# Query and key chunks of the input projection: one 512-column product for both halves of x, partial sums added on VectorE, bias preparation in other units

## What is computed

```python
xn = rms_norm(h, ln1_w)
proj = xn @ w_in          # 9 chunks of 512 columns: q, k, v of 3 attention groups; then GLA q, k, v, gate; merge gates
o_a = dilated_mixer(a_qkv)
o_b = gla_mixer(gq, gk, gv, gog, glr, w_gk2, b_gk2, gla_norm_w)
mixed = gate_a * (o_a @ w_proj_a) + gate_b * (o_b @ w_proj_b)
h = h + mixed @ w_out
h = h + moe_ffn(rms_norm(h, ln2_w), ...)      # top 4 of 32 experts, each 1024 -> 2048 -> 1024
```

## Time and profile before

| | us |
|---|---|
| three runs, median (lowest to highest) | 1250.7 (1250.55 to 1251.64) |
| span of the profiled execution, first to last instruction | 1248.5 |
| TensorE busy | 1169.1 (94%) |
| VectorE busy | 445.6 (36%) |
| ScalarE busy | 250.3 (20%) |
| GpSimd busy | 15.9 (1%) |

### The profile page before, as it was taken

How to read it: one execution, slowest core, us unless ns; L and a number is a source line. 1 busy time by engine, 2 the same in 40 slices (tenths; PEclk the granted TensorE clock), 3 DMA queues, 4 the chain that set the end, 5 groups by cost and what they waited for, 6 DMA issues and landing times.

```text
span 1248.5 us, 17019 instructions
## 1 busy us (share of the span) xinstructions
PE 1169.1 (94%) x7215; PEld 604.2 (48%) x7216; DVE 445.6 (36%) x766; ACT 250.3 (20%) x353; POOL 15.9 (1%) x30
## 2 busy tenths in 40 slices
PE   9999999999999999899899989898989989899997
PEld 9998988888633343333333333333333333333332
DVE  5754546666532233222222222222322222222232
ACT  4544445544401010001000000000000001000012
POOL 2200000000000000000000000000000000000000
PEclk9999999999999999999999999999999999999999
DMA  9645333377999999999999999999999999999996
GB/s 296 219 169 186 135 135 135 135 277 282 371 417 425 431 431 427 430 430 429 431 433 427 431 430 429 430 430 434 433 428 431 433 427 431 435 427 432 421 428 278
DMA packets 50031, 456.98 MB, mean 366 GB/s; under 512 B 5988, under 2 KB 6136, under 8 KB 31400
## 3 DMA queue, kind: packets, MB, share of 16 engines
q1 hardware_dynamic: 49544, 455.09, 87.7%
q10 hardware_dynamic: 448, 1.32, 0.3%
HBM read 455.35 MB, written 1.05 MB: 366 GB/s over the span
## 4 chain that ended last, share of the span: by engine, by line
PE 59%; DMA 35%; DVE 2%; SPq 2%; ACT 1%; issue 1%; DVEq 0%
PE ps L1384 57%; DMA ring<-in_w_up_dram 22%; DMA arena<-in_w_up_dram 12%; PE ps L1891 1%; DMA ring<-in_w_in_dram 1%; ACT w_split L588 0%; SPq L397 0%; DVE w_split L892 0%; SPq L399 0%; PE ps L1777 0%; PE ps L1573 0%; SPq L414 0%; DVE arena L1062 0%; SPq L391 0%; PE ps L1680 0%
## 5 line engine op out<-in xcount | busy, mean ns | idle before, releaser
L1384 PE MATMUL ps<-ring,arena 128*64 128x512 f32 x2304 | 523.2, 608 | 50.9 <-DMA ring<-in_w_up_dram 50.9
L1384 PEld LDWEIGHTS ps<-ring,arena 128*64 128x64 f32 x2304 | 163.9, 140 | 378.8 <-issue 300.3
L1384 PE MATMUL ps<-arena 128*64 128x512 f32 (+3 forms) x920 | 202.7, 563 | 17.0 <-DMA arena<-in_w_up_dram 16.1
L1296 DVE TENSOR_SCALAR arena<-ps 128x512 f32<-128x512 f32 x32 | 22.1, 692 | 487.3 <-PE ps L1384 487.3
L892 DVE TENSOR_TENSOR w_split<-ring,w_split 128x2048 fp32r<-128x2048 f32 x48 | 109.8, 2291 | 108.4 <-ACT w_split L588 108.1
L1384 PEld LDWEIGHTS ps<-arena 128*64 128x64 f32 (+1 forms) x920 | 78.2, 149 | 128.4 <-issue 100.2
L796 ACT ACTIVATE arena<-arena 128x512 f32<-128x512 f32 x32 | 20.2, 631 | 552.6 <-DVE arena L1296 552.6
L1384 PE MATMUL ps<-w_split,x_split 128*128 128x512 f32 x528 | 123.5, 392 | 0.7 <-ACT arena L624 0.5
L1384 PEld LDWEIGHTS ps<-w_split,x_split 128*128 128x128 f32 x528 | 98.4, 188 | 21.8 <-issue 1.2
L588 ACT ACTIVATE w_split<-ring 128x2048 fp32r<-128x2048 f32 x47 | 89.6, 1911 | 70.7 <-PE ps L1384 62.5
L1384 PE MATMUL ps<-x_split,w_split 128*128 128x256 f32 x768 | 94.7, 284 | 0.1
(11 more groups left out here) (251 smaller groups left out, 624.8 us busy)
## 6 DMA issues: line engine op xcount, KB each, us to landing
ring<-in_w_up_dram SPq DMA_DIRECT2D x40, 4096.0 KB, 31.1
ring<-in_w_down_dram SPq DMA_DIRECT2D x46, 2048.0 KB, 30.2
arena<-in_w_up_dram SPq DMA_DIRECT2D x14, 4096.0 KB, 31.1
ring<-in_w_in_dram SPq DMA_DIRECT2D x17, 2048.0 KB, 7.8
arena<-in_w_down_dram SPq DMA_DIRECT2D x14, 2048.0 KB, 30.0
ring<-in_w_up_dram SPq DMA_DIRECT2D x12, 2048.0 KB, 23.1
arena<-in_w_up_dram SPq DMA_DIRECT2D x4, 2048.0 KB, 23.5
ring<-in_w_up_dram SPq DMA_DIRECT2D x8, 1024.0 KB, 8.7
```

The costliest lines, as they stand in the source:

```text
L1296: dve.tensor_scalar(glu_c, ps[bank][:, :], LIMIT, None, ALU.min).then_inc(glu_ok, 1)
L1384: return pe.matmul(dst, lhsT, rhs, start=start, stop=stop, skip_group_check=True)
```

## The change

1. The two halves of x lie side by side for each k tile: `x_both` is [P, KT, 2, SEQ]; `x_split` is the same memory with the axes swapped back.
2. In the seven chunks 1, 3, 4, 6, 7, 9, 10 (`by_weights`, 14 units) the high weights multiply both halves of x in one matmul of 512 columns, into a whole bank: columns 0 to 255 hold high x high, 256 to 511 high x low. Low weights x high x is a second matmul of 256 columns into the first half of the bank. A unit of chunks 3 to 10 so fills two banks, ps[0] and ps[1], one for each of its two groups of 128 columns (m), and the next unit uses the same two (`bank_free`). Chunk 1 uses ps[2] to ps[5].
3. VectorE adds the two halves of a bank and writes the result (`halves_added`, TENSOR_REDUCE, 256 sums of two), 28 of them; ScalarE's 14 copies of these chunks go. `halves_added(u)` stands ahead of w_low(u+3).
4. The bias preparation stands in other units: pieces of u = 6 and 7 in 10, of 8 in 11, of 9 in 16, and the small split of 10 in 12. Those of u = 4 and 5 stay.
5. The semaphore `warmed`, on which nothing waits, goes.

```diff
+        x_both = nc.alloc_sbuf_tensor_at("x_split", [P, KT, 2, SEQ], F32R, offset=slot_at[DENSE_RING])
+        x_split = x_both[:, :, :, :].rearrange("p k i t -> p i k t")
...
+        def by_weights(u):
+            return u // 2 == 1 or (u // 2 < QKV_CHUNKS + 2 and u // 2 not in BY_ROWS)
...
+        def dve_outs(u):
+            return sum(2 for v in range(u) if by_weights(v))
...
                 if u == 5:
                     then(dve.tensor_tensor(bias_f, bias_f, bias_p[0:E, :], ALU.subtract))
-                if u == 6:
+                if u == 10:
                     then(dve.tensor_copy(tmp_b, bias_f))
-                if u == 7:
                     dve.tensor_copy(bias_p[E:2 * E, :], tmp_b)
-                if u == 8:
+                if u == 11:
                     then(dve.tensor_tensor(bias_f, bias_f, tmp_b, ALU.subtract))
-                if u == 9:
+                if u == 16:
                     dve.tensor_copy(bias_p[2 * E:3 * E, :], bias_f).then_inc(pick_ok, 1)
-                if u == 10:
+                if u == 12:
                     dve.wait_ge(glr_in, 32)
...
+            def halves_added(u):
...
+                for m in range(2):
+                    if m == 0:
+                        dve.wait_ge(tile_done, halves_done(u))
+                    else:
+                        dve.wait_ge(proj_done, u + 1)
...
+                    dve.tensor_reduce(dst, ps[m].rearrange("p (i t) -> p t i", i=2), AX_X, ALU.add).then_inc(added, 1)
...
+            def bank_free(u, b):
+                if by_weights(u - 1) and u != 4:
+                    pe.wait_ge(added, dve_outs(u) - 1 + b)
+                else:
+                    pe.wait_ge(proj_out, act_outs(u) - 1 + b)
...
-                if u >= 2:
-                    pe.wait_ge(proj_out, u - 1)
                 for m in range(2):
-                    dst = ps[u % 2][:, m * SEQ:m * SEQ + SEQ]
+                    bank_free(u, m)
                     for k in range(KT):
-                        ins = product(dst, [split_w(u, i)[:, k, m * P:m * P + P] for i in range(2)],
-                                      [x_split[:, i, k, :] for i in range(2)], k == 0, k == KT - 1)
-                ins.then_inc(proj_done, 1)
+                        w = [split_w(u, i)[:, k, m * P:m * P + P] for i in range(2)]
+                        mm(ps[m], w[0], x_both[:, k, :, :].rearrange("p i t -> p (i t)"), k == 0, False)
+                        ins = mm(ps[m][:, 0:SEQ], w[1], x_split[:, 0, k, :], False, k == KT - 1)
+                    ins.then_inc((tile_done, proj_done)[m], 1)
```

More of the change, by code:

```diff
@@ L263, in layer @@
         res_ok = [sem(f"res_ok{t}") for t in range(TT)]
-        wo_half, part_ok, sel0_ok, xin_half_ps, xin_half_ok, warmed = (
-            sem(n) for n in ("wo_half", "part_ok", "sel0_ok", "xin_half_ps", "xin_half_ok", "warmed"))
+        wo_half, part_ok, sel0_ok, xin_half_ps, xin_half_ok = (
+            sem(n) for n in ("wo_half", "part_ok", "sel0_ok", "xin_half_ps", "xin_half_ok"))
         lg_ps, lg_shift, lg_exp, taken_ok, count_ps, turns_ok = (
@@ L316, in split_w, with act_outs, tiles_before, halves_done @@
             return w_split[:, u % SPLITS, part, :].rearrange("p (k n) -> p k n", k=tiles)
+        def by_weights(u):
+            return u // 2 == 1 or (u // 2 < QKV_CHUNKS + 2 and u // 2 not in BY_ROWS)
+        def act_outs(u):
+            return sum(1 for v in range(u) if not by_weights(v))
+        def dve_outs(u):
+            return sum(2 for v in range(u) if by_weights(v))
+        def tiles_before(u):
+            return sum(1 for c in BY_ROWS if c < u // 2) + sum(1 for v in range(4, u) if by_weights(v))
+        def halves_done(u):
+            return tiles_before(u) + 1
         def tiles_done(c):
-            return BY_ROWS.index(c) + 1
+            return tiles_before(2 * c) + 1
         O_BANK = ((5, 2), (6, 7))
@@ L625, in projection_out @@
                     return
-                if c < DENSE_RING:
+                if c == 0:
                     if s == 0:
@@ L636, in projection_out @@
                     return
[L637 to L648, removed]
             def mix_high(j):
@@ L1084, in gate_products @@
                        .then_inc(gl_ops, 1)
+            def halves_added(u):
+                c, s = u // 2, u % 2
+                if c == 1:
+                    if s:
+                        for m in range(4):
+                            if m < 2:
+                                dve.wait_ge(tile_done, tiles_done(c))
+                            else:
+                                dve.wait_ge(proj_done, u + 1)
+                            dve.tensor_reduce(qkT[:, 1, 0, m, :], ps[2 + m].rearrange("p (i t) -> p t i", i=2),
+                                              AX_X, ALU.add).then_inc(added, 1)
+                    return
+                for m in range(2):
+                    if m == 0:
+                        dve.wait_ge(tile_done, halves_done(u))
+                    else:
+                        dve.wait_ge(proj_done, u + 1)
+                    if c < QKV_CHUNKS:
+                        dst = qkT[:, c % 3, c // 3, 2 * s + m, :]
+                    else:
+                        if u == 2 * C_GQ and m == 0:
+                            dve.wait_ge(pick_ok, 1)
+                        dst = (gqT if c == C_GQ else gkT)[:, s * 512 + m * SEQ:s * 512 + m * SEQ + SEQ]
+                    dve.tensor_reduce(dst, ps[m].rearrange("p (i t) -> p t i", i=2), AX_X, ALU.add).then_inc(added, 1)
             for u in range(UNITS):
+                if by_weights(u):
+                    halves_added(u)
                 if U_PB <= u < U_WO and (u - U_PB) % 2:
@@ L1470, in projection @@
                     for m in range(4):
-                        if first and m % 2 == 0:
-                            pe.wait_ge(proj_out, m // 2 + 1)
                         for k in range(4):
                             kk = 4 * (u % 2) + k
-                            ins = product(ps[m // 2][:, m % 2 * SEQ:m % 2 * SEQ + SEQ],
-                                          [split_w(u, i)[:, k, m * P:m * P + P] for i in range(2)],
-                                          [x_split[:, i, kk, :] for i in range(2)], kk == 0 and m % 2 == 0, kk == KT - 1)
+                            w = [split_w(u, i)[:, k, m * P:m * P + P] for i in range(2)]
+                            mm(ps[2 + m], w[0], x_both[:, kk, :, :].rearrange("p i t -> p (i t)"), kk == 0, False)
+                            ins = mm(ps[2 + m][:, 0:SEQ], w[1], x_split[:, 0, kk, :], False, kk == KT - 1)
                         if m == 1 and not first:
@@ L1484, in projection @@
                     for t in range(TT):
-                        if first and u + t >= 2:
-                            pe.wait_ge(proj_out, u + t - 1)
+                        if first:
+                            bank_free(u, t)
                         for k in range(4):
@@ L1556, in at_scores @@
                 if h == 0:
-                    pe.wait_ge(proj_out, 2 * QKV_CHUNKS)
+                    pe.wait_ge(proj_out, act_outs(2 * QKV_CHUNKS))
+                    pe.wait_ge(added, dve_outs(2 * QKV_CHUNKS))
                 for g in range(NG):
```

21 lines of the change are left out of this document (11 added, 10 removed).

## The result

| | kernel before | changed kernel |
|---|---|---|
| median of five runs each, us | 1250.55 (1250.23 to 1251.64) | 1260.61 (1259.12 to 1261.22) |
| ratio, 95% interval | | 1.0073 (1.0062 to 1.0084) |
| span of the profiled execution, us | 1248.5 | 1259.5 |

The change costs 10.1 us; 7.7 were forecast. In a later session (experiment 11) it was 1262.93 against 1250.81, ratio 1.0093 (1.0073 to 1.0112), so 12.1 us.

What follows compares the result with a forecast made beforehand. TensorE was taken to bound the projection, transfers the experts, with dense-part losses carried to the end. Gain -2.2, waits +6.9 and slow clock +3.0 gave +7.7 us on 1250.7: 1258.4 us, range 1254.0 to 1262.0.

Steps and rivals of the forecast that it cites:

- Cost 3: Units 6 and 12: sums stand behind 3.34 us bias subtractions on VectorE, so TensorE idles 3.5 and 3.4 us, 6.9 together.
- Cost 2: VectorE's sums take 0.69 us each and fit in plain query units with 0.3 us left over.
- the rival of double sums: VectorE's sums cost 1.38 us each, lengthening both waits and adding waits in plain steps: 3.0 us more, 1261.4; chance 0.10.
- Cost 1: TensorE's projection matmuls: two per k tile, not three, save 0.20 us a unit in eleven units, 2.2 us gained.
- Cost 4: TensorE's clock falls to half behind the two new waits, 1.5 us each, 3.0 in all; bounds 0 and 3.5.
- Waits without the slow clock: Projection: both waits come but TensorE stays at 2.4 GHz; +4.7 us, 1255.4; chance 0.14.
- Taken up behind the projection: Between late unit 7 and the first expert transfer the projection's loss vanishes, so not slower: 1250.7; chance 0.07.
- The sum passes the subtraction: VectorE, unit 6: first sum done by 51.6, not late, so only the 2.2 us gain remains: 1248.5; chance 0.07.

Runs made afterwards that it cites:

- experiment 11: Also after_again: the changed kernel run once more, unaltered, for a second profile; 1262.93 us, ratio 1.0093 to the kernel before.
- natural_slots: Experiment 1: changed kernel with first bias subtraction moved from u = 5 to 9, second from u = 11 to 15; 1249.75 us, ratio 0.9989 to the kernel before.
- second_moved: Experiment 2: changed kernel with only the second bias subtraction moved, from u = 11 to u = 15; 1254.35 us in one execution.
- experiment 4: Kernel before with the bias preparation in the units of the change and nothing else; 1250.84 us, ratio 1.0001.
- experiment 5: Changed kernel with units 7, 9, 13 and 15 using banks ps[2] and ps[3]; 1249.29 us, ratio 0.9987 to the kernel before.
- Experiment 3: Also filler: changed kernel with 44 small unread matmuls in front of units 7 and 13; 1256.34 us, ratio 1.0046 to the kernel before.
- experiment 10: Kernel before with only the new layout of x_split; 1250.71 us, ratio 0.9999.
- experiment 8: Changed kernel with bias subtractions moved to u = 9 and 15, and five late-wanted small loads issued behind chunk 2; 1248.70 us, ratio 0.9982 to the kernel before.
- old_slots: Changed kernel with the bias preparation where it stood before the change; 1257.29 us in one execution.
- before_late: Kernel before with only the five late-wanted small loads issued behind chunk 2; 1250.37 us, ratio 0.9996.

## Why the prediction was right, point by point

- **Cost 3, the two waits: right, in place, cause and size.** Forecast 3.5 and 3.4 us in front of units 7 and 13; measured 3.32 and 3.25. Experiments 1, 2, 4 and 5 show the cause from four sides. The start of a late unit against before, less unit 4's shift, is +3.34 and +3.29; the forecast's 55.05 for unit 7 had 3.29 in it.
- **Cost 2, the sums: right.** 0.69 was taken from the 512-column rows, 0.688 measured; the strided pairs cost nothing extra, and the rival of double sums fell. No wait came in front of units 8, 9, 14 and 15, with the 0.3 us left over.
- **Cost 1, the gain: right in sign, too large.** Forecast 0.20 us per unit. In natural_slots, free of waits, units 6 to 9 take 22.46 in place of 23.03 and units 12 to 15 22.70 in place of 23.03: 0.14 and 0.08. The step that failed is "both widths agree on the fixed cost", from which I took the wide rate and the narrow one to add up in a mixed stream. They do not: a pair took 351 and 355 ns in these stretches, not 347.3. From the start of unit 4 to the first expert transfer the eleven units gained 1.2 us in all (227.86 against 229.03), where 2.2 were forecast, and regrouping brought back 0.2 to 0.5. The Trainium skill, TensorE: Matmul & The Clock Gate, section "Wait — 56ns, not 53.3ns?", has a fixed cost of about 2.5 ns per matmul; by it the gain would have been 0.04 per unit, and the measured one lies between that and the row's. That the gain of unit 18 goes into the softmax wait was right: the wait grew from 1.00 to 1.19, and from unit 18's start to the transposes it is 7.09 us, against 7.10 before.
- **Cost 4, the clock: right mechanism, mis-sized.** 3.0 us forecast, with 3.5 as the bound; 4.4 in the first profile, 3.1 in the second, all of it in units 13 to 15 (19.77 us, where units 7 to 9 took 16.72 at full clock; TensorE worked 6.12 of the 6.83 us). The step that failed is the bound: I priced a slow stretch by the one cost in the earlier trace rows, 1.75 us, and a stretch can cost more: beside the ones of 3.41 us there are two of 6.83 us on record, which cost 2.7 and 3.1. Experiment 3 puts the term at about 4 us in the first session's median. As the same wait drew 0, 3.41 and 6.83 us of slow clock, a forecast of one number here can only be near by luck.
- **What I gave nothing:** unit 4 began 0.71 us later. The forecast had it at 34.95. Of the eight profiles that have the new products and the old load order seven show it late (35.45 to 36.15), the three with the old products and that order do not (34.75 to 34.95). In the seven the second half of chunk 1 already lands 0.6 to 1.0 us late (19.31 to 19.64 against 18.67). The eighth, filler, has the same products and hardly shows it (18.78, unit 4 at 35.12), so the new products do not always bring it. It is not the layout (experiment 10) and not the moved pieces (experiment 4). The SP queue shows where the time goes, in the issue of the small load router_b, ahead of chunk 2:

```profile
14.82 4.99 SPq L399 DMA_DIRECT2D router_b<-in_b_router_dram  x1
```

```profile
14.53 6.17 SPq L421 DMA_DIRECT2D router_b<-in_b_router_dram  x1
```

  The first is the kernel before, the second the changed one. It lasts 5.7 to 6.2 us in the seven, 4.8 to 5.1 in the three, 3.97 in filler. Why it lasts longer stays open; in experiment 8, where chunk 2 goes first, unit 4 no longer depends on it. The expert stage's +0.7 is within what that stretch varies between the profiles (984.1 to 985.9, those of the last section left out).
- **Rivals.** "Waits without the slow clock" happened behind single waits (old_slots, after_again's first), but no execution of the changed kernel came near its 1255.4: the lowest of nine is 1259.12. "Taken up behind the projection" fell: the first expert transfer moved by 10.26 of the 11.0. "The sum passes the subtraction" fell: each began right behind it.

Sum by the forecast's steps: waits less gains 4.7 forecast, measured 3.34 - 0.77 + 3.29 - 0.43 - 0.32 = 5.1; clock 3.0, measured 4.4; unit 4 and the experts 0, measured 1.4. Together 7.7 and 11.0 in spans (the parts rounded); in medians, 10.1. All three parts came out above the forecast, so its total was not near by errors that cancel; the clock and what I gave nothing make up most of the difference.

## What to carry to other kernels

If work moves from one engine to another that takes its instructions in order, look at what stands ahead of it there: a side job that was free as long as nobody waited behind it becomes a wait of up to its whole length (3.32 us of 3.34 here, 2.00 of 3.34 in front of old_slots' unit 10, none behind its cast). A bank that is wanted again half a step after it was filled needs a reader with no long instruction ahead; more banks or another place for the long instruction are equally good cures. And a wait of TensorE is to be priced with what follows it, here 4 us of slow clock for 6.6 us of waits.

## What the runs showed of the hardware that was not expected

The same wait, 3.32 us long to the digit and at the same place in front of unit 7, was followed by 6.83 us at half clock in one execution (the changed kernel's first profile), 3.41 in another (second_moved) and none in two (after_again, old_slots). Behind waits of 2 to 3 us among the experts it was the same in the changed kernel's profile:

```profile
526.67 7.09 PE L1421 MATMUL ps<-ring,arena 128*64 128x512 f32 x32 [2.63 <-DMA ring<-in_w_up_dram]
...
555.91 8.78 PE L1421 MATMUL ps<-arena 128*64 128x512 f32 x32 [2.63 <-DMA arena<-in_w_up_dram]
```

So the length of a wait does not settle whether the clock falls, and one profile is one draw. The Trainium skill, TensorE: Matmul & The Clock Gate, Part 1, has an idle array fall to half its clock; the runs agree that it happens behind waits, and add that it need not.

A second draw of that kind has nothing to do with the change: in the profiles of natural_slots and before_late the clock was at half for 10.24 us from 328.3 on, in the router's stretch of short matmuls and short waits, and these executions were some 4 us longer than their kernels' medians (1253.71 against 1249.75, 1253.92 against 1250.37). Windows of natural_slots, and behind them the same window of the kernel before:

```profile
328.40:338.40 10.00, 10.00 (x39) 0.50 0.57 240
```

```profile
328.40:338.40 10.00, 9.93 (x61) 1.00 0.88 345
```

39 matmuls in 10 us, against 61. The kernel before has single executions of 1254.3 to 1255.9 in each of the three sessions of the experiments as well; whether they are of this kind, no profile of it shows.
